# One layer of a two-block network: mLSTM with all chunk states first, and its gates, maxima and convolution inside the row projections

## The reference, cut to what matters

```
naq, nak, nav, mlqk, mlv, mlo, mlg = split(h @ w_in)      # 512,512,512,1024,512,512,16 columns
na   = neighbourhood_attention(naq, nak, nav, bias)       # 8 heads of 64
q,k  = split(silu(conv3(mlqk)));  q *= 128**-0.5          # 4 heads of 128
i, f = mlg + gate_b  (one pair forwards, one backwards);  logf = log_sigmoid(f)
# mLSTM, in chunks of 128 tokens, state (C, n, m), context first, then latent:
bcum = cumsum(logf);  d_in = bcum[t] - bcum[s] + i[s]  where s <= t
m_t  = max(bcum + m_st, max_s d_in);  w = exp(d_in - m_t);  a = exp(bcum + m_st - m_t)
qk   = (q @ k.T) * w
num  = a * (q @ C.T) + qk @ v;   den = a * (q @ n) + sum(qk)
h    = num / max(|den|, exp(-m_t))
C,n,m = decay*C + (wk*v).T @ k,  decay*n + sum(wk*k),  m_new
# once per direction (the second on reversed tokens), then
ml   = headwise_norm(sigmoid(mlo) * (h_fwd + h_bwd)) * g
y    = concat(na, ml) @ w_out
```

## Time and profile before

| | us |
|---|---|
| three timed runs | 3511.84, 3515.91, 3516.82 |
| median | 3515.91 |
| the profiled execution | 3519.12 |
| its span, first to last instruction | 3517.3 |
| TensorE busy | 2994.1 |
| VectorE busy | 1923.0 |
| ScalarE busy | 1386.5 |

### The profile page before, as it was taken

The page is one execution under the profiler, slowest core; times in us unless marked ns, Lnnn a source line. Parts: engine busy times, 40 slices in busy tenths (PEclk is TensorE's granted clock), DMA queues, the critical chain, the costliest instruction groups (busy, mean ns, idle before and its releaser), DMA issues. The chain is left out here.

```text
span 3517.3 us, 38747 instructions
## 1 busy us (share of the span) xinstructions
PE 2994.1 (85%) x15404; PEld 2293.2 (65%) x15404; DVE 1923.0 (55%) x2286; ACT 1386.5 (39%) x1777; POOL 13.5 (0%) x13
## 2 busy tenths in 40 slices
PE   6999599785999999999997897866469989749797
PEld 4798498674766766766765443555457767617795
DVE  3555544155878878878884200255544543335575
ACT  3210344143666666666663100130043333224554
POOL 0000000000000000000000000000000000000000
PEclk9998799896999999999998898886589999879898
DMA  4300255323988989989998923100012222100352
GB/s 156 120 1 1 90 186 181 119 96 132 355 340 335 351 322 344 350 329 344 348 348 333 420 88 87 49 1 0 3 48 84 96 84 84 68 30 1 120 180 84
DMA packets 95183, 590.04 MB, mean 168 GB/s; under 512 B 20608, under 2 KB 21632, under 8 KB 25632
## 3 DMA queue, kind: packets, MB, share of 16 engines
q1 hardware_dynamic: 90688, 576.60, 43.7%
q10 hardware_dynamic: 4320, 10.99, 0.9%
HBM read 586.50 MB, written 1.05 MB: 167 GB/s over the span
## 5 line engine op out<-in xcount | busy, mean ns | idle before, releaser
L1801 DVE TENSOR_TENSOR s_w_low<-weight_ring,s_w_high 128x2048 fp32r<-128x2048 f32 x336 | 759.7, 2290 | 136.8 <-ACT s_w_high L1740 132.9
L1740 ACT ACTIVATE s_w_high<-weight_ring 128x2048 fp32r<-128x2048 f32 x336 | 629.9, 1909 | 139.1 <-PE bank L1721 116.5
L242 DVE TENSOR_TENSOR s_w_low<-weight_ring,s_w_high 128x1024 fp32r<-128x1024 f32 x238 | 289.4, 1222 | 200.0 <-ACT s_w_high L227 199.9
L1721 PE MATMUL bank<-s_w_high,s_x_low 128*96 128x512 f32 x896 | 364.2, 406 | 7.6 <-DVE s_w_low L1801 7.6
L484 PE MATMUL bank<-s_x_high,s_w_low 128*128 128x256 f32 (+1 forms) x1056 | 341.1, 323 | 29.4 <-DVE s_w_low L242 29.4
L227 ACT ACTIVATE s_w_high<-weight_ring 128x1024 fp32r<-128x1024 f32 x238 | 249.6, 1052 | 283.0 <-PE bank L484 282.9
L1721 PE MATMUL bank<-s_w_high,s_x_high 128*96 128x512 f32 x896 | 359.1, 401 | 0.0
L1721 PE MATMUL bank<-s_w_low,s_x_high 128*96 128x512 f32 x896 | 357.3, 399 | 0.0
L484 PE MATMUL bank<-s_x_low,s_w_high 128*128 128x256 f32 (+1 forms) x1056 | 339.7, 322 | 0.0
L484 PE MATMUL bank<-s_x_high,s_w_high 128*128 128x256 f32 (+1 forms) x1056 | 339.2, 321 | 0.0
L338 PE MATMUL bank<-s_w_high,s_x_low 128*128 128x512 f32 x544 | 220.1, 405 | 57.0 <-DVE s_w_low L242 57.0
(11 more groups left out here) (403 smaller groups left out, 4396.1 us busy)
## 6 DMA issues: line engine op xcount, KB each, us to landing
weight_ring<-moe_w SPq DMA_DIRECT2D x336, 1024.0 KB, 6.6
weight_ring<-ada_w SPq DMA_DIRECT2D x48, 1024.0 KB, 12.8
weight_ring<-ffn_up SPq DMA_DIRECT2D x44, 1024.0 KB, 4.8
weight_ring<-ffn_w_in SPq DMA_DIRECT2D x22, 1024.0 KB, 4.8
weight_ring<-ffn_down SPq DMA_DIRECT2D x22, 1024.0 KB, 4.8
weight_ring<-ffn_w_down SPq DMA_DIRECT2D x11, 1024.0 KB, 4.8
weight_ring<-w_rkv_cols SPq DMA_DIRECT2D x8, 1024.0 KB, 7.9
weight_ring<-moba_qk SPq DMA_DIRECT2D x8, 1024.0 KB, 4.8
```

What stands on the lines that cost most here:

```text
L242: K.nc.vector.tensor_tensor(self.lo[:, b, :], self.source(c, i), self.hi[:, b, :], ALU.subtract)\
L1721: last = nc.tensor.matmul(o, xs[:, e % 2, k, :], ws[:, b, c], start=(k == 0 and m == 0), stop=(k == KT - 1 and m == 2))
L1740: nc.scalar.activation(halves(whi, kind, n, i), raw(kind, n, i), ACT.Copy).then_inc(S["high"].h, 1)
L1801: V.tensor_tensor(halves(wlo, kind, n, i), raw(kind, n, i), halves(whi, kind, n, i), ALU.subtract)\
```

## The change

`stream` issues the small loads of `K.later` ahead of the weight chunks. `linear_rows512`, the block of the gates, the convolution's block, the transposes of k, the block of the gain's load, the norm's block and the last transposes go; two blocks take their place, `mlstm_gates` before the attention and a new `mlstm` after it.

`mlstm_gates` does the row projection with one set of four banks, evacuated by ScalarE (the output gate through Sigmoid); the gate matmuls stand first on TensorE; the convolution, the gates and all running maxima (by a doubling of distances over a transposed row of 16 partitions) stand beside the projection on VectorE and ScalarE; the coefficients of all four chunks are ready at its end.

`mlstm` forms the three states first, then the outputs. Scores are computed transposed (k by q), once per tile for both directions, so that the weights need no transposes; the mask is added by a matmul; the row sums are matmuls of one column.

```
 def stream(self, sp):
+        for dst, src in self.later:
+            load(self, sp, dst, src)
+        self.later = []
         while self.issued < min(self.taken + R, len(self.plan)):
...
-        for dst, src in self.later:
-            load(self, sp, dst, src)
-        self.later = []
...
+# mlstm_gates, TensorE (after the 32 gate matmuls)
+            for m in range(3):
+                if m:
+                    pe.wait_ge(*kept.at(m))
+                for c in range(2):
+                    w = K.chunk(pe).rearrange("p (k n) -> p k n", k=4)
+                    for k in range(4):
+                        for tt in range(4):
+                            last = nc.tensor.matmul(K.ps[tt][:, :], hT[:, 4 * c + k, tt * P:(tt + 1) * P], w[:, k, :], ...)
+                    last.then_inc(*K.used.up())
+                    if (m, c) == (0, 1):   # cumulative sums: 3 matmuls, after asked.at(3)
...
+                    if (m, c) == (1, 0):   # 2 transposes of u8, after u_made.at(1)
...
+                    if (m, c) == (2, 0):   # 2 transposes and 2 matmuls of the maxima, after peaked.at(1)
...
+# mlstm_gates, VectorE: bias + window, tap(0..3), gates, tap(4..7), sums, u8, 7 doublings, coefficients
+            for n in range(7):
+                a, b = run[n % 2], run[(n + 1) % 2]
+                for d in range(2):
+                    far = slice(64 - (1 << n), 192 - (1 << n)) if d == 0 else slice(1 << n, 128 + (1 << n))
+                    last = V.tensor_tensor(b[:, d, data[d]], a[:, d, data[d]], a[:, d, far], ALU.max)
+                K.v(dve, last)
...
+# mlstm_gates, ScalarE: silu(0..3), Exp, Ln, silu(4..7), scale of q, keep(0), keep(1), Exp of args, keep(2)
+            def keep(m):
+                act.wait_ge(*K.used.at(2 * m + 2))
+                for tt in range(4):
+                    last = nc.scalar.activation(outs[m][:, tt, :], K.ps[tt][:, :], ACT.Sigmoid if m == 2 else ACT.Copy)
+                K.a(act, last, kept)
...
+# mlstm, TensorE
+            def row(i):
+                for d in range(2):
+                    pe.wait_ge(*spread.at(2 * i + d + 1))
+                    if i:
+                        pe.wait_ge(*weights.at(2 * i + d - 1))
+                    nc.tensor.matmul(K.ps[d][:, :], K.ones[:, :], diag[:, i % 2, d, :], start=True, stop=False)
+                    nc.tensor.matmul(K.ps[d]..., K.ident[:, :], bc(mask[:, 1 - d, :]...), start=False, stop=True)
+            def apply(i):
+                pe.wait_ge(*weighted.at(i + 1))
+                pe.wait_ge(*(read.at(i) if i else grown.at(3)))
+                for d in range(2):
+                    for h in range(4):
+                        matmul(ps[3 + d][head h], W[i, d, h], vrow[tt, head h])      # 128 columns
+                        matmul(ps[7][one column], W[i, d, h], ones[:, 0:1])          # 1 column
+                        if step[i][d]:
+                            matmul(ps[5 + d][head h], cqk[h, cols(tt)], C[k][d, h])  # 128 columns
+                            matmul(ps[7][one column], cqk[h, cols(tt)], ns[k, d, h]) # 1 column
...
+            for tt in (2, 3, 0, 1):
+                turn(tt)                    # 4 transposes each
+            row(0); grow(0); grow(1)        # grow: 8 matmuls of 128 columns
+            total(); score(0)               # total: 24 of one column; score: 4 of 128
+            row(1); grow(2); score(1)
+            row(2); row(3)
+            for i in range(4):
+                apply(i)
+                if i + 2 < 4:
+                    score(i + 2)
+            ...                             # 4 x 4 transposes of the normed rows
+# mlstm, VectorE: mix(i), after small operations on den; scaled adds out of the banks
+                K.v(dve, V.reciprocal(den, den), scaled)
+                dve.wait_ge(*mixed.at(i + 1))         # ScalarE: four scaled copies of bank 3
+                for bank, d, s in ((5, 0, far), (4, 1, den), (6, 1, far)):
+                    if bank == 4 or step[i][d]:
+                        for h in range(4):
+                            last = V.scalar_tensor_tensor(z[h], K.ps[bank][:, head(h)], s[:, d, h:h + 1], z[h], ALU.mult, ALU.add)
+                        K.v(dve, last, read if ... else None)
...
+            sp.dma_start(mg, K.i["ev_ml_norm_g"].partition_broadcast(P)).then_inc(*gain_in.up(16))
+            K.stream(sp)
```

More of the change, by code:

```diff
@@ L84, in __init__ @@
             "placed")}
+        self.gating = {n: Sig(sem(f"gating_{n}")) for n in (
+            "gated", "asked", "given", "summed", "u_made", "u_turned", "peaked", "peaks_back", "args_made", "tapped",
+            "active", "rows_kept")}
+        self.scan = {n: Sig(sem(f"scan_{n}")) for n in (
+            "spread", "broad", "weights", "scored", "keyed", "added", "grown", "weighted", "summed", "scaled", "mixed",
+            "read", "turned", "norm_ask", "norm_root", "normed", "flipped", "placed", "gain_in")}
         self.ps = [ctx.enter_context(nc.psum_tensor(f"bank{b}", [P, 512], F32)) for b in range(8)]
@@ L2212, in conv_ffn @@
         linear_rows(K, hid, range(FC // P), None, tts=tts, tail=lambda s: passage(K, s, x, tts, gates, nxt, room))
[L2215 to L2244, removed]
 def even_layer(K, x4, hT, gates, nxt):
@@ L2273, in even_layer @@
                     zero=naq[:, :, :])
-        linear_rows512(K, hT, [nav, mlv, mlo])
-        G8, lf, tmp, bb, tot, u8 = scratch(K, inner, [P, 4, 2, 2, 4], *[[P, 4, 2, 4]] * 5)
+        G8, lf, tmp, bb, tot, u8 = scratch(K, inner, [P, 2, 4, 2, 4], *[[P, 2, 4, 4]] * 5)
+        args, = scratch(K, inner, [P, 6, 2, 4, 4])
         SEQ = ((2, 3, 0, 1), (3, 2, 1, 0))
[L2277 to L2329, removed]
@@ L2331, in even_layer @@
-        neighbourhood(K, naq, nak, nav, bias, yT, (hT[:, 0:4, :], hT[:, 4:8, :]))
[L2334 to L2345, removed]
-            @block.scalar
-            def _(act):
-                for j in range(KT):
-                    act.wait_ge(*cv.at(j + 1))
-                    K.a(act, nc.scalar.activation(cqk[:, j, :], cqk[:, j, :], ACT.Silu))
-                K.a(act, nc.scalar.activation(cqk[:, 0:4, :], cqk[:, 0:4, :], ACT.Copy, scale=P ** -0.5))
-                K.a(act, nc.scalar.activation(mlo[:, :, :], mlo[:, :, :], ACT.Sigmoid))
-            @block.sync
-            def _(sp):
-                K.stream(sp)
@@ L2366, in even_layer @@
-        sqrts = K.sig(2)
-        with K.begin() as block:
-            @block.vector
-            def _(dve):
-                K.v(dve, V.tensor_tensor(hf, hf, hb, ALU.add))
-                K.v(dve, V.tensor_tensor(hf, hf, mlo, ALU.mult))
-                for tt in range(4):
-                    z = hf[:, tt, :].rearrange("p (n w) -> p n w", n=4)
-                    layer_norm(K, dve, z, z, (st_, mv, rs), mg[:, :], None, P, 4, EPS, sqrts)
-            @block.scalar
-            def _(act):
-                roots(K, act, *sqrts, [rs[:, :]] * 4)
-            @block.sync
-            def _(sp):
-                K.stream(sp)
@@ new lines, in mlstm @@
+    S = K.scan
+    for s in S.values():
+        s.base = s.n
+    spread, broad, weights, scored, keyed, added, grown, weighted, summed, scaled, mixed, read, ask, rooted, normed, flipped, placed = (
+        S[n] for n in ("spread", "broad", "weights", "scored", "keyed", "added", "grown", "weighted", "summed", "scaled",
+                       "mixed", "read", "norm_ask", "norm_root", "normed", "flipped", "placed"))
+    gain_in, turned = S["gain_in"], S["turned"]
+    flat = lambda a: a.rearrange("p j t -> p (j t)")
@@ new lines, in mlstm @@
+    den, neg, far = (small[:, n:n + 8].rearrange("p (d h) -> p d h", d=2) for n in (544, 552, 560))
+    st = small[:, 576:600].rearrange("p (h s) -> p h s", h=4)
+    mv = small[:, 600:632].rearrange("p (i h s) -> p i h s", i=4, h=4)
+    rs = small[:, 632:648].rearrange("p (i h) -> p i h", i=4)
+    order = (2, 3, 1, 0)
+    home = (2, 7, 5, 6)
+    step = [[SEQ[d].index(tt) for d in range(2)] for tt in order]
+    later, never, decay, write, negmu = (args[:, n] for n in range(5))
+    cols = lambda tt: slice(tt * P, (tt + 1) * P)
```

442 lines of the change are left out of this document (323 added, 119 removed).

## The result

The changed kernel takes 3395.26 us (median of 4 runs, 3394.44 to 3396.15) against 3513.88 us (4 runs, 3510.01 to 3516.82): the ratio is 0.9663, with a 95% interval of 0.9646 to 0.9680. The forecast was 3401. The profiled execution took 3394.44 us, its span is 3391.4 us.

The account below looks back on a forecast made before the run. It took TensorE, busy 85% of 3517.3 us, to bound the kernel. Terms -24.0, -0.5 and -90.5 sum to -115: 3404.1 from the profiled execution, 3401 us after allowing for its 3.2 above the median; range 3377 to 3430.

Parts of the forecast that it names:

- S: Stretch from the column projection's first matmul to the output projection's first; the forecast's whole gain of 115 us lies there.
- The stall: TensorE's 25.73 us idle after the column projection, while SyncE issues 39 small loads; 1.7 us would remain, term -24.0.
- rival C: Ahead of the row projection the barrier stall stays, through VectorE, ScalarE or a late weight: +24, 3425 us; chance 0.04.
- The merged phase: Gates phase and row projection in one: 107.6 us in place of 108.1, convolution, gates and maxima costed at nothing; term -0.5.
- rival D: In the gates and projection phase, gates, convolution and maxima aren't fully covered: +15, 3416 us; chance 0.06.
- The scan phase: Convolution to norm replaced by one phase after the attention: 123.5 us in place of 214.0, term -90.5.
- (a): Scan phase's head up to the first `apply`, partly at half clock: 40 us; all full 30, all half 56.
- (b): The four `apply` of the scan phase, 112 matmuls at half clock less a warm beginning: 45 us; all full 27.
- (c): Gaps between the applies, `mix` up to `read`: 5.1, 5.1, 6.6 and 9.2, together 26 us; bounds 21 and 32.
- (d): Norm at the scan phase's end: root with its table load, four tiles, last transposes and copy, 11.5 us.
- Rival B: The scan phase's head serialises on ScalarE, the clock stays low, `mix` at its upper bound: +26, 3427 us; chance 0.17.
- Rival A: The scan phase runs warm, its head and applies losing 25 us more: 3376 us; chance 0.12.

Follow-up runs that it names:

- experiment 1: The kernel before with only the small loads issued ahead of the weight chunks: 3490.12 us against 3519.49, ratio 0.9920.
- experiment 2: The changed kernel with the small loads put back behind the weight loop of `stream`: 3418.00 us, ratio 0.9716 to the kernel before.
- experiment 4: The changed kernel with the convolution in a block of its own ahead of the merged one: 3413.92 us, ratio 0.9698 to the kernel before.
- experiment 7: The changed kernel with the gate matmuls behind the row projection's first chunk, not ahead of it: 3386.25 us, ratio 0.9632 to the kernel before.
- experiment 10: The changed kernel with two rows between applies, gate matmuls behind the first chunk, six useless matmuls before the last apply: 3371.91 us, ratio 0.9587 to the kernel before.
- experiment 12: The kernel of experiment 10 with `row(1)` moved ahead of the one-column sums: 3368.14 us, ratio 0.9577 to the kernel before.
- experiment 3: The changed kernel with VectorE's convolution operations and ScalarE's Silu each issued twice: 3399.99 us, ratio 0.9662 to the kernel before.
- experiment 6: The changed kernel with four useless 512-column matmuls after each of the first three applies: 3379.75 us, ratio 0.9621 to the kernel before.
- experiment 9: The changed kernel with the 32 one-column row sums of the weights done twice: 3407.32 us, ratio 0.9682 to the kernel before.

## Why the prediction was right

It put S at 115 us less, and 122.6 were found. The mechanisms were the ones named in it; the sizes were off by more than the total shows, as one term fell short by 2 us and others went beyond theirs by 10. The stretch from the end of the column projection to the output projection, 298 us by its own test, took 290.9 (2136.1 to 2427.0), inside its 270 to 325. By its steps:

**The stall** (-24.0): 25.73 to 1.71, exact. Experiments 1 and 2 show its cause, SyncE's issues, and that rival C did not happen.

**The merged phase** (107.6 forecast): 2137.85 to 2247.55 is 109.7. The gate matmuls took 13.3 to the start of the next (12.5), the waits for `kept` 1.63 + 2.21 = 3.8 (4.5), the end 3.9 (4.1). What was off most is the wide matmuls with the small products among them: 88.6 us where 84.5 + 2 was forecast, as the first matrix starts cold behind the narrow gate matmuls (clock 0.92) and the third ran its first chunk in 15.70 in place of 14.00 (0.94). The forecast had the waits in the sum and no clock cost beside them. For the third matrix the wait of 2.21 by itself is not the cause: in experiments 2, 4, 7, 10 and 12 the same wait is followed by a chunk of 14.00. The convolution, gates and maxima at nothing were right: ScalarE had 13.78 us left. Experiment 3 shows what my rival D would have cost, and experiment 4 that the cover saves 20 us of wait. How much of the gain comes from the maxima by doubling alone was not tried.

Of the table loads, ScalarE's timeline shows:
```profile
2243.68 1.28 ACT L2401 ACT_TABLE_LOAD   x1 [9.38 <-PE bank L2301]
2244.98 2.06 ACT L2401 ACTIVATE s<-bank 128x512 f32<-128x512 f32 x4
...
2410.77 1.28 ACT L2688 ACT_TABLE_LOAD   x1
...
2416.58 0.22 ACT L2688 ACTIVATE s<-s 128x16 f32<-128x16 f32 x1 [4.53 <-DVE s L2643]
```
The Sigmoid's activation starts 0.02 us behind its load of 1.28; there is no sign of the drain of 1.38 us that the Trainium skill, "ScalarE: Activation LUTs", What ACT_TABLE_LOAD costs, would add, and to leave it out was right. The root's load was done 4.5 us ahead of the operand that the activation waits for, so the norm did not pay for it.

**The attention** (0): 64.8 against 65.5.

**The scan phase** (123.5 forecast): 114.7. (a) The head took 34.4, not 40: this is the largest error, a term mis-sized. The four rows came to 15.7 (17.6 forecast), the small matmuls behind them to 15.5 (17.2), the transposes to 3.2 (3.9), and the 1.5 of waits did not occur. The head's clock is 0.81, more than my "half at full, half not" supposed. In TensorE's timeline the 24 sums, of two instructions each, take 7.53 us, 0.31 each, where half and half would be 0.335. The row, and two windows of it:
```profile
2323.02 7.53 PE L2517 MATMUL bank<-ones,s 128*128 128x1 f32 x48
```
```profile
2323.00:2326.00 3.00, 3.00 (x30) 3.00 (x28) 0.00 (x0) 0.11 (x1) 0.00 (x0) 1.00 0.00 0
2326.00:2330.40 4.40, 4.40 (x22) 4.40 (x23) 0.00 (x0) 0.00 (x0) 0.00 (x0) 0.50 0.00 0
```
The clock fell in the middle of the sums, with TensorE busy all the time: not only gaps let it fall. The head's forecast, wide matmuls that start cold and narrow ones that lose the clock again, has this mechanism; its share at half was too high.

(b) The applies took 5.3 + 10.25 + 13.7 + 13.7 = 42.9, against 45: the first is wholly warm and the others cold. (c) The gaps between them were 5.5, 5.4, 6.7 and 8.6 = 26.2, against 5.1, 5.1, 6.6 and 9.2 = 26. The one price with no row, the scaled add of 128 columns, held: VectorE's timeline has 12 of them in 3.45 us, 0.29 each, where 0.28 was taken.
```profile
2390.43 3.45 DVE L2606 SCALAR_TENSOR_TENSOR s<-bank,s 128x128 f32<-128x128 f32 x12 [1.01 <-ACT s L2684]
```
(d) The norm took 10.1 of 11.5, the difference being the root's table load.

Rival B (the head serialises) fell: TensorE is busy 34.38 of the head's 34.40 us. Rival A (warm) came true for a part: the head, at 0.81, and the first apply are 5.6 and 2.1 us under their terms, where it had 25 for all; the other three applies are cold. Each of the cold applies follows idle time of 3.4 to 6.6 us, and experiment 6 shows that wide matmuls in those gaps give back 12.5 us. The narrow matmuls by themselves did not raise the clock, 13.7 us of them without a pause stay at 0.50, nor did they hold it in the sums above and in the third apply of experiment 10. The Trainium skill, "TensorE: Matmul & The Clock Gate", Part 1, says that sustained matmul activity releases the throttle; the rows agree for the wide matmuls only.

The time was missed by 5.7 us: S by 7.6 and the rest of the span by 3.3, less 1.2 outside the span and 4.0 by which the profiled executions stand to their medians (3.2 above it before, 0.8 below it after). That the time came out closer than S is luck. One reading of the page was incomplete: the tenth of its 40 slices stands at 6 tenths too, in a stage that the change doesn't touch.

## What to carry to other kernels

Find out first which gaps are nobody's work: 39 small loads issued at the end of a block were worth 24 us and three moved lines, and it could be read off one queue's timeline. Price a chain of narrow fp32 matmuls at half clock if each link follows a gap, and see whether useful wide matmuls of the same phase can be moved into the gaps; here two rows moved so were worth 12.4 us, a tenth of what the whole change brought, of which 5.2 was the moved work and the rest the clock; four matmuls of no use in each gap gave as much. Look at what the moved work stood ahead of, too: the first apply lost 4.0 us of clock by it. What is hidden under a dense phase has a slack that can be read (here the 13.78 us of ScalarE); work that overruns it costs its delay and may cost clock behind it. And before a few us are put down to an edit, see whether stretches that it leaves alone stayed the same: here such stretches moved by 1.4 and 1.7 us.

## What was not expected of the hardware

- TensorE went faster with work added: 24 more instructions of 512 columns, and S 12.5 us shorter, as the matmuls behind them ran at clock 1.00 in place of 0.50 (experiment 6).
- An fp32 matmul of one column costs what one of 128 columns does: 0.427 us at half clock, 0.22 at full (experiment 9).
- The clock fell from 1.00 to 0.50 in the middle of 24 one-column matmuls, with TensorE busy throughout (2323.0 to 2330.4 in the changed kernel).
- Behind a wait of TensorE that grew from 1.63 to 5.46 us, the dense stretch took another 2.9 us (clock 0.90 in place of 1.00, experiment 3; one trace).
- The same instructions behind the same wait of 2.2 us took 15.70 us in some traces and 14.00 in others (first chunk of the third matrix).
- A table load ran ahead of the wait of its activation and was done 4.5 us before the operand was there (L2688). Not every load does: the Sigmoid's (L2401) began only when its bank was ready, after 9.38 us of idle time of ScalarE, and stood on the path with its 1.28 us.
